# A state-space mixer in fp32: the states' turned parts go to the output product unsummed, and the second broadcast of scales is made later

## The reference

```python
uf = u.reshape(bsz, length, N_GROUPS, SSM_GROUP)          # 64 groups of 16 channels
lam_bar = exp(lam * dt)                                   # 64 complex states per group
bu = einsum('blgc,gpc->blgp', uf, ((lam_bar - 1) / lam)[..., None] * b)
_, states = lax.associative_scan(_ssm_binop, (a_elems, bu), axis=1)
y = real(einsum('blgp,gcp->blgc', states, c)) + d_skip * uf
z = gelu(y)
zw = z @ w_glu
return zw[..., :D_MODEL] * sigmoid(zw[..., D_MODEL:])
```

## Time and profile before

| | |
|---|---|
| median of 3 runs | 2156.45 us (2152.4 to 2157.42) |
| the profiled execution | 2157.53 us |
| its span in the profile | 2155.7 us |
| busy PE, DVE, POOL, ACT | 1979.7, 1110.4, 1047.3, 733.4 us |
| mean granted clock of TensorE | 0.974 of full speed |
| the mixer's chunks | about 922 to 1034.6 us of the span |

### The profile page before, as it was taken

The page is one execution under the profiler, slowest core; times in us unless marked ns, Lnnn a source line. Parts: engine busy times, 40 slices in busy tenths (PEclk is TensorE's granted clock), DMA queues, the critical chain, the costliest instruction groups (busy, mean ns, idle before and its releaser), DMA issues.

```text
span 2155.7 us, 30205 instructions
## 1 busy us (share of the span) xinstructions
PE 1979.7 (92%) x9963; PEld 1603.1 (74%) x9963; DVE 1110.4 (52%) x1820; ACT 733.4 (34%) x1233; POOL 1047.3 (49%) x573
## 2 busy tenths in 40 slices
PE   7888998989999999756899999999997799999997
PEld 5677766768887888545778888887876678888886
DVE  6787873654678696689434223132137844132232
ACT  4323234353322322435442222233235643222223
POOL 5465425526765744680454444446444235444442
PEclk9999999999999999889999999999999999999999
DMA  4233002323332333100233333334345413333332
GB/s 142 71 91 100 1 1 64 98 50 88 97 98 85 94 95 90 56 2 0 69 98 98 89 105 90 98 97 99 97 111 124 112 59 97 98 98 92 103 88 88
DMA packets 343417, 179.52 MB, mean 83 GB/s; under 512 B 27951, under 2 KB 335527, under 8 KB 343335
## 3 DMA queue, kind: packets, MB, share of 16 engines
q1 hardware_dynamic: 342592, 177.81, 29.4%
q10 hardware_dynamic: 742, 0.68, 0.1%
HBM read 162.73 MB, written 2.10 MB: 76 GB/s over the span
## 4 chain that ended last, share of the span: by engine, by line
PE 54%; issue 12%; POOL 9%; DVE 9%; POOLq 6%; DVEq 4%; ACT 4%; DMA 2%; SPq 1%; ACTq 0%
PE ACC L1436 15%; PE ACC L1442 15%; PE ACC L1437 15%; POOL WL L1113 7%; POOLq L1123 2%; DVEq L2222 1%; POOLq L1295 1%; POOLq L1283 1%; DVE PTL L2228 1%; ACT WH L550 1%; DMA RAW<-in_w_v_cross_dram 1%; PE ST L1558 1%; PE ST L1560 1%; PE ST L1559 1%; PE O L1558 1%
## 5 line engine op out<-in xcount | busy, mean ns | idle before, releaser
L1113 POOL TENSOR_TENSOR WL<-RAW,WH 128x1024 fp32r<-128x1024 f32 (+1 forms) x308 | 733.4, 2383 | 792.3 <-ACT WH L550 717.7
L1436 PE MATMUL ACC<-PH,WH 128*128 128x512 f32 x1248 | 495.6, 397 | 11.7 <-DVE PL L1962 3.1
L1437 PE MATMUL ACC<-PL,WH 128*128 128x512 f32 x1248 | 489.5, 392 | 0.0
L550 ACT ACTIVATE WH<-RAW 128x1024 fp32r<-128x1024 f32 (+1 forms) x308 | 317.8, 1034 | 490.1 <-PE ACC L1442 414.4
L1436 PE MATMUL ACC<-QH,WH 128*128 128x512 f32 (+1 forms) x1136 | 431.5, 384 | 23.8 <-ACT WH L550 18.1
L1437 PE MATMUL ACC<-QL,WH 128*128 128x512 f32 (+1 forms) x1136 | 426.8, 380 | 0.0
L1442 PE MATMUL ACC<-PH,WL 128*128 128x512 f32 x1248 | 311.1, 391 | 0.0
L1436 PEld LDWEIGHTS ACC<-PH,WH 128*128 128x128 f32 x1248 | 236.5, 190 | 71.1 <-issue 4.7
L1442 PE MATMUL ACC<-QH,WL 128*128 128x512 f32 (+1 forms) x1136 | 272.3, 380 | 9.6 <-POOL WL L1113 9.4
L1437 PEld LDWEIGHTS ACC<-PL,WH 128*128 128x128 f32 x1248 | 236.6, 190 | 49.3 <-issue 1.0
L1442 PEld LDWEIGHTS ACC<-PH,WL 128*128 128x128 f32 x1248 | 234.0, 188 | 52.6 <-issue 3.3
(11 more groups left out here) (416 smaller groups left out, 2436.0 us busy)
## 6 DMA issues: line engine op xcount, KB each, us to landing
RAW<-in_mlp_w_dram SPq DMA_DIRECT2D x128, 512.0 KB, 4.0
RAW<-in_w_gate_dram SPq DMA_DIRECT2D x22, 512.0 KB, 3.7
RAW<-in_w_up_dram SPq DMA_DIRECT2D x22, 512.0 KB, 3.7
RAW<-in_w_in_dram SPq DMA_DIRECT2D x16, 512.0 KB, 3.8
RAW<-in_w_down_dram SPq DMA_DIRECT2D x16, 512.0 KB, 4.0
RAW<-in_ssm_w_glu_dram SPq DMA_DIRECT2D x16, 512.0 KB, 3.8
RAW<-in_w_kvf_dram SPq DMA_DIRECT2D x16, 512.0 KB, 3.9
RAW<-in_w_k_cross_dram SPq DMA_DIRECT2D x8, 512.0 KB, 4.0
```

Of the source, the lines that this page charges most:

```text
L550: act.activation(WH[:, s, 0:kc], RAW[:, s, 0:kc], ACT.Copy).then_inc(w_hi, 1)
L1113: pool.tensor_tensor(WL[:, s, 0:kc], RAW[:, s, 0:kc], WH[:, s, 0:kc], ALU.subtract).then_inc(w_lo, 1)
L1436: pe.matmul(ACC[s][:, 0:n], WH[:, s, k, :], xh[:, k, :], start=(k == 0), stop=False)
L1437: pe.matmul(ACC[s][:, 0:n], WH[:, s, k, :], xl[:, k, :], start=False, stop=False)
```

## The change

What the output product needs is the complex product of state and table, summed. Its two halves are no longer summed on VectorE: TURNA holds the real part of the states times (cosine, sine), TURNB the imaginary part times (minus sine, cosine), and the output product runs over both, adding in PSUM. So the drain and two sums go, the second product is replaced by two of half its size, and the output product has 64 matmul instructions in place of 32, of 127 columns each. sp_ready counts two per chunk. SPV and its memset go; GC moves to make room.

The second broadcast (DIAG to RS) is moved: VectorE makes DIAG behind the first two UN and copies RS ahead of the first `turned_in`; TensorE broadcasts behind the first `state_inputs`, into ACC[0] in place of ST, and waits for the copy.

```diff
-        SPV = at("SPV", [P, 2, 4, NM], F32, 32768)
+        TURNA = at("TURNA", [P, 2, 4, NM], F32, 32768)
+        TURNB = at("TURNB", [P, 2, 4, NM], F32, 45056)
...
-        GC = at("GC", [P, 2, LAG + 1, 4, 16], F32, 45056)
+        GC = at("GC", [P, 2, LAG + 1, 4, 16], F32, 77824)
...
-                        act.wait_ge(sp_ready, KC)
+                        act.wait_ge(sp_ready, 2 * KC)
...
-            spread_scales("final")
...
-                pe.wait_ge(sp_ready, c + 1)
-                for i in range(LAG):
-                    for ri in range(2):
-                        for j in range(4):
-                            mm = pe.matmul(Y[32 * j:32 * j + 32, i, :],
-                                           CL[b][:, ri, i + 1, j].rearrange("p a b -> p (a b)"), SPV[:, ri, j, :],
-                                           start=False, stop=(ri == 1 and i == LAG - 1), skip_group_check=True)
+                for k, of in enumerate((TURNA, TURNB)):
+                    pe.wait_ge(sp_ready, 2 * c + k + 1)
+                    for i in range(LAG):
+                        for ri in range(2):
+                            for j in range(4):
+                                mm = pe.matmul(Y[32 * j:32 * j + 32, i, 1:NM],
+                                               CL[b][:, ri, i + 1, j].rearrange("p a b -> p (a b)"), of[:, ri, j, 0:NM - 1],
+                                               start=False, stop=(k == 1 and ri == 1 and i == LAG - 1), skip_group_check=True)
                 mm.then_inc(y_mm, 1)
 
             state_inputs(0, 0)
+            pe.wait_ge(st_diag, NORM["final"] + 1)
+            pe.matmul(ACC[0][:], ONES, DIAG[:], start=True, stop=True).then_inc(st_bc, 1)
+            pe.wait_ge(st_rs, NORM["final"] + 1)
             mixer(0, 0, True)
...
-                        dve.memset(SPV[:, :, :, 0], 0.0)
...
-            for to, r, ready in ((DIAG2, R8[:, TB:2 * TB], diag2), (DIAG, R8[:, 0:TB], st_diag)):
-                dve.tensor_tensor(to[:].rearrange("p (b t) -> p b t", b=TB), IDENT[:, None, :].to_broadcast([P, TB, P]),
-                                  r[:, :, None].to_broadcast([P, TB, P]), ALU.mult).then_inc(ready, 1)
+            def diagonal_of(to, r):
+                return dve.tensor_tensor(to[:].rearrange("p (b t) -> p b t", b=TB), IDENT[:, None, :].to_broadcast([P, TB, P]),
+                                         r[:, :, None].to_broadcast([P, TB, P]), ALU.mult)
+
+            diagonal_of(DIAG2, R8[:, TB:2 * TB]).then_inc(diag2, 1)
             dve.wait_ge(bc2, 1)
             dve.tensor_copy(RS2[:], SB[3])
-            dve.wait_ge(st_bc, NORM["final"] + 1)
-            dve.tensor_copy(RS[:], ST[:]).then_inc(st_rs, 1)
             dve.drain()
...
-                turned(WR[:, :, :, 0:n], ET[:, 0, four, 0:n], ET[:, 1, four, 0:n], n)
-                dve.drain()
-                dve.tensor_tensor(SPV[:, 0, :, 1:NM], RTC[:, 0, :, 0:n], RTS[:, 1, :, 0:n], ALU.subtract)
-                dve.tensor_tensor(SPV[:, 1, :, 1:NM], RTC[:, 1, :, 0:n], RTS[:, 0, :, 0:n], ALU.add).then_inc(sp_ready, 1)
+                dve.tensor_tensor(TURNA[:, :, :, 0:n], WR[:, 0, :, 0:n][:, None].to_broadcast([P, 2, 4, n]),
+                                  ET[:, :, four, 0:n], ALU.mult).then_inc(sp_ready, 1)
+                dve.tensor_tensor(TURNB[:, 1, :, 0:n], WR[:, 1, :, 0:n], ET[:, 0, four, 0:n], ALU.mult)
+                dve.scalar_tensor_tensor(TURNB[:, 0, :, 0:n], WR[:, 1, :, 0:n], -1.0, ET[:, 1, four, 0:n],
+                                         ALU.mult, ALU.mult).then_inc(sp_ready, 1)
                 dve.drain()
...
             for c in range(2):
                 chunk_in(c, c)
+            diagonal_of(DIAG, R8[:, 0:TB]).then_inc(st_diag, 1)
+            dve.wait_ge(st_bc, NORM["final"] + 1)
+            dve.tensor_copy(RS[:], ACC[0][:]).then_inc(st_rs, 1)
             turned_in(0)
```

## The result

The changed kernel took 2141.64 us in the median of 4 runs (2138.74 to 2144.84), the kernel before 2156.66 (4 runs, 2152.4 to 2157.42): ratio 0.9933, 95% interval 0.9918 to 0.9948. The three intervals have only 0.9945 to 0.9948 in common, 11.2 to 11.9 us.

A forecast was written before the change was run, and what follows sets the result against it. VectorE's order of work was taken to set the mixer's length, stretched by GpSimd up to chunk 2. Terms -8.5 - 2.2 + 0.4 + 0.3 = -10.0 us gave 2146.5 us, range 2142.5 to 2152.5.

The forecast's parts named there:

- VectorE's part, 7 x 1.22 = 8.5 us: Mixer, VectorE: fewer and smaller instructions save 1.22 us per chunk, passed on by seven chunks, 8.5 us.
- the two ends kept: Chunks 0 to 2, beside GpSimd's weight making: VectorE saves between 1.22 and about 1.7 us per chunk.
- Two passes at the full clock, 3.7 us, hidden: Output product on TensorE: both passes take 3.7 us and end 0.5 us before VectorE needs the result.
- ScalarE's loop, +0.4: End of mixer: loop over product, UC and L1850, 11.6 us, outlasts VectorE's 11.34; charged 0.4 us (0 to 1.0).
- The decisive product length of the rival (4.7 us): Loop over UC, L1850 and product: a product above 4.7 us makes it longer than today's 12.6; rival's chance 0.05.
- The last chunk, -2.2: Last chunk, start to YC: 4.97 us in place of 7.14, saving 2.2; 0.8 with the first pass at half clock.
- The moved broadcast, +0.3 (0 to 1.0): Mixer's start: RS's copy, waiting for the broadcast, stands ahead of the first turning; charged +0.3 us (0 to 1.0).
- the 1.7 us won are spent again: Mixer's start: UN begins 1.7 us sooner, but first turning starts at 922.1 to 923.0 against 922.03 us.
- The sum, -10.0: Whole kernel: -8.5 - 2.2 + 0.4 + 0.3 = -10.0 us, giving 2146.5 us.
- with 1.5 us for the spread of the median (the runs lie 5 us apart): Range's lower end: 1.5 us allowed for the median's spread beyond the most that can be saved, giving 2142.5 us.
- Both rivals on TensorE's clock: Output product: first pass at half clock everywhere, 2154 us, chance 0.13; both passes at half clock, 2162.5 us, chance 0.05.

The follow-up runs named there:

- the third pass: Changed kernel with TURNB's pass of the output product made twice, output not the reference's: 2150.03 us, ratio 0.9987 to the kernel before.
- same: The kernel before run once more without any edit, as a control: 2153.76 us beside 2154.28, ratio 0.9994.
- turn_only: Changed kernel with the second broadcast back in its old place: 2144.38 us, ratio 0.9954 to the kernel before.
- third_time: The changed kernel run a third time without any edit: 2144.59 us beside 2153.34 for the kernel before, ratio 0.9960.
- rs_last: Changed kernel with the second broadcast moved into the last chunk, ahead of the output product: 2142.75 us, ratio 0.9958 to the kernel before.
- one_wait: Changed kernel, but both passes of the output product wait for TURNB: 2144.93 us beside 2152.67 for the kernel before, ratio 0.9967.

## Why the prediction was right or wrong

The mechanism was right and the time was missed: 2141.6 us where the range began at 2142.5. The changed kernel came out 4.8 us under the forecast. Of these, 1.4 us are the mixer's (11.4 for a sum of 10.0) and 3.6 us arose outside it; 0.2 go back because the kernel before came out that much higher than in the runs that the prediction had.

- **VectorE's part, 7 x 1.22 = 8.5 us.** Measured 9.3 (97.2 to 87.9 us for chunks 0 to 6). The scalar_tensor_tensor cost 0.68 us, the cheap end of what was allowed, which makes it 1.28 to 1.29 a middle chunk. The three early ones gave 4.1 us, between the two ends kept (3.7 and 5.1); between other profiles of the two kernels it was up to 5.5. This term was too small: in the means of the two and three profiles the seven chunks gave 9.9 us.
- **Two passes at the full clock, 3.7 us, hidden.** 3.68 us in chunk 4, over 1.2 us before YC. L1850 was over 1.9 us after TURNA's start, not 2.5, because the product ahead of its loop had ended sooner; the product was over at 5.5, not 6.2. In chunk 0 the first pass did run at half clock (3.50 us after a stand of 3.71) and was hidden. The prediction tied the clock of a pass to how long TensorE had stood, from three passes; a fourth, chunk 4's (2.98 us, full clock), is not among them and contradicts it. The passes of the new order, which stood little, did run at the full clock as forecast, but the reason given is not shown by the rows.
- **ScalarE's loop, +0.4.** In the changed kernel's first profile it is 11.43 us in chunk 4, and VectorE's 11.48. In chunk 5 it is 11.44 against 11.28, but L1850 had begun 0.26 us ahead of TURNA and was still ahead behind it: no charge. The loop itself was shown by the third pass, which made it the bound at the length worked out. The decisive product length of the rival (4.7 us) was right in kind: at 5.4 us a middle chunk is longer (13.2) than before the change (12.8).
- **The last chunk, -2.2.** Measured 2.1; against the profile of same, whose last product ran partly at the full clock (2.69 us), 1.5.
- **The moved broadcast, +0.3 (0 to 1.0).** 0.7 to 1.3 us later to the first turning than in the profile of before, 1.1 to 1.6 later than in turn_only. The broadcast took 1.54 us and not 1.0, and L1850 ahead of it 3.80 and not 3.40. By chunk 0's start it is 0.0 in the first pair of profiles and 0.8 against turn_only, up to 1.7 in third_time, beyond the 1.0 allowed. The step "the 1.7 us won are spent again" was right, and rs_last showed why.
- **The sum, -10.0.** Mixer to mixer 11.4 us in the first pair of profiles; 10.9 between the means of the two kernels' profiles (123.0 and 112.2). In times 15.0, 9.6 and 8.8 us. The means by part are -9.9 for chunks 0 to 6 (-8.5 + 0.4 were forecast), -1.8 for the last (-2.2) and +0.8 ahead of chunk 0 (+0.3).

The step that failed is the one that turned the sum into a range: "with 1.5 us for the spread of the median (the runs lie 5 us apart)". Its size was wrong. The mixer's 11.4 us alone would have given a time within the range. Outside the mixer the two medians differed by another 3.6 us, which did not come again. Executions of the kernel before lie from 2144.7 to 2163.4 us over all runs made here, and medians of 4 to 25 of them came to 2152.7 to 2156.7. The first comparison had the kernel before 2 to 4 us higher than later ones and the changed one 3 us lower. Three runs within 5 us of each other did not show that. From the two sides together some 4 us had to be allowed, not 1.5 (an estimate from the difference of 15.0 and 10.9 us).

Why both sides of the first comparison lay so far out isn't shown. Chance alone is a thin account: pairs of medians of four, drawn from the later executions (71 of the kernel before, 13 of the changed one), differ by 4.5 to 13.1 us in 95 of 100 draws, and by 15.0 or more in fewer than one (an estimate from the times on record). Later comparisons ran on different chips, with 2152.7 to 2154.3 us for the kernel before, and nothing was run to tell a chip's or an occasion's share from that of single executions. What the first pair of profiles does show is where the difference of these two executions lies: ahead of the mixer, where TensorE's clock differed at several places. The changed kernel's 903.0 us there were the rarer case.

Both rivals on TensorE's clock did not come about: the clock is 1.00 in every window from chunk 3 on. The one pass that followed a stand of 2.5 us at full clock (one_wait) does not show how near they were, for passes of the kernel before ran at half clock after 2.57 and at full after 2.98 us.

## What to carry to other kernels

Where one engine sets the pace and another stands idle beside it, sums can go to the matrix engine as further accumulating passes, as long as the loop through the other engines stays under the first one's. Work that loop out too: it says how much may be moved. A broadcast that is not needed yet is best put where both of its engines already wait, and not merely behind the first thing it delays; here that was worth 1.8 us of the mixer. And a range must hold the difference of two medians, not only the effect: take the spread from many executions, or allow for it.

## What the runs showed of the hardware

TensorE's granted clock fell to half in a stretch in which it was busy without a pause (204 to 212 us of the profile of before), after eight microseconds with pauses of at most 0.45 us. It did so in ten profiles of thirteen, and not in each of the same code. The parts ahead of the mixer were 906.0 to 911.2 us with it and 903.0 to 904.4 us without. The Trainium skill, TensorE: Matmul & The Clock Gate, Part 1, lets activity release the clock; this stretch, full before and after and half in between with 4.00 of 4.00 us busy, is not explained by that alone. How long TensorE had stood did not decide the clock of the next pass: half after 2.57 and 2.96 us, full after 2.76 and 2.98. The scalar_tensor_tensor with two inputs in SBUF took 0.68 us for 508 elements, no more than the plain product of that size.
